# Output norm of the delta rule: square sums formed inside the scan, reciprocals on packed rows

## The reference, cut to what matters

```
def rms_norm(x, gain):
    y = xf * lax.rsqrt(jnp.mean(xf * xf, axis=-1, keepdims=True) + EPS)
    return (y * gain.astype(jnp.float32)).astype(x.dtype)

    o = gated_delta_rule(q, k, v, beta, g).transpose(0, 2, 1, 3)
    zf = z.reshape(b_, s_, GDN_HEADS, GDN_DV).astype(f32)
    o = rms_norm(o, o_gain) * jax.nn.silu(zf)
    return o.reshape(b_, s_, GDN_VDIM).astype(hn.dtype) @ w_out
```

## Time and profile before

| | us |
|---|---|
| median of 3 runs | 2438.69 (2437.46 to 2439.86) |
| profiled execution, its own time | 2455.42 |
| its span, from first to last instruction | 2453.6 |
| TensorE busy | 2096.4 (85%) |
| VectorE busy | 1113.7 (45%) |
| ScalarE busy | 697.3 (28%) |
| GpSimd busy | 319.3 (13%) |
| mean granted TensorE clock, share of full | 0.921 |

### The profile page before, as it was taken

How to read it: one execution, slowest core, us unless ns; L and a number is a source line. 1 busy time by engine, 2 the same in 40 slices (tenths; PEclk the granted TensorE clock), 3 DMA queues, 4 the chain that set the end, 5 groups by cost and what they waited for, 6 DMA issues and landing times. The chain is left out here.

```text
span 2453.6 us, 26623 instructions
## 1 busy us (share of the span) xinstructions
PE 2096.4 (85%) x10044; PEld 1566.1 (64%) x10044; DVE 1113.7 (45%) x1530; ACT 697.3 (28%) x1021; POOL 319.3 (13%) x299
## 2 busy tenths in 40 slices
PE   5988994878878996899929999997897658999999
PEld 2766762322246774788817888885675436788887
DVE  3433333111135678665483544334487343544333
ACT  2331131111124443112123322222443452422222
POOL 1331011111123430323101000000000110100000
PEclk9998696999989998899969999999998879999999
DMA  8155026999931221000002333331221002333331
GB/s 314 52 184 187 1 69 262 418 424 423 417 142 48 90 86 51 1 1 1 1 17 79 93 103 94 94 99 56 77 77 52 0 0 69 94 95 96 95 100 52
DMA packets 61937, 283.12 MB, mean 115 GB/s; under 512 B 9984, under 2 KB 11296, under 8 KB 52512
## 3 DMA queue, kind: packets, MB, share of 16 engines
q1 hardware_dynamic: 53072, 266.95, 30.9%
q0 software_dynamic: 6256, 11.03, 1.2%
q10 hardware_dynamic: 2528, 4.01, 0.5%
HBM read 280.90 MB, written 14.68 MB: 120 GB/s over the span
## 5 line engine op out<-in xcount | busy, mean ns | idle before, releaser
L307 PE MATMUL ps<-ff_hhi,ff_whi 128*128 128x512 f32 x704 | 276.9, 393 | 8.5 <-DVE ff_hlo L2486 8.3
L2404 DVE TENSOR_TENSOR ff_wlo<-ring,ff_whi 128x1024 fp32r<-128x1024 f32 x132 | 163.4, 1238 | 247.5 <-ACT ff_whi L2400 247.5
L309 PE MATMUL ps<-ff_hlo,ff_whi 128*128 128x512 f32 x704 | 275.4, 391 | 0.0
L308 PE MATMUL ps<-ff_hhi,ff_wlo 128*128 128x512 f32 x704 | 275.4, 391 | 0.0
L2400 ACT ACTIVATE ff_whi<-ring 128x1024 fp32r<-128x1024 f32 x132 | 139.2, 1055 | 321.7 <-PE ps L309 299.9
L1451 PE MATMUL ps<-w_up,hgT 128*64 128x512 f32 x576 | 145.2, 657 | 45.4 <-DMA w_up<-experts 45.4
L307 PEld LDWEIGHTS ps<-ff_hhi,ff_whi 128*128 128x128 f32 x704 | 133.2, 189 | 38.2 <-DVE ff_wlo L2404 10.2
L308 PEld LDWEIGHTS ps<-ff_hhi,ff_wlo 128*128 128x128 f32 x704 | 133.2, 189 | 28.1 <-issue 0.5
L309 PEld LDWEIGHTS ps<-ff_hlo,ff_whi 128*128 128x128 f32 x704 | 133.0, 189 | 27.9
L307 PE MATMUL ps<-ff_ahi,ff_whi 128*128 128x512 f32 x352 | 136.9, 389 | 0.0
L308 PE MATMUL ps<-ff_ahi,ff_wlo 128*128 128x512 f32 x352 | 136.9, 389 | 0.0
(11 more groups left out here) (553 smaller groups left out, 4135.1 us busy)
## 6 DMA issues: line engine op xcount, KB each, us to landing
ring<-stream SPq DMA_DIRECT2D x276, 512.0 KB, 3.6
w_up<-experts SPq DMA_DIRECT2D x36, 2048.0 KB
mix<-experts SPq DMA_DIRECT2D x18, 1024.0 KB, 19.9
hn<-experts SPq DMA_DIRECT2D x18, 1024.0 KB, 21.1
yrow<-y_dram SPq DMA_DIRECT2D x4, 1024.0 KB, 8.0
tab<-table POOLq DMA_DIRECT2D x1, 2528.5 KB, 12.3
res<-xT ACTq DMA_DIRECT2D x1, 2048.0 KB, 18.6
h_dram<-mix SPq DMA_DIRECT2D x4, 512.0 KB, 11.3
```

Of the source, the lines that this page charges most:

```text
L307: pe.matmul(out, w_hi, a_hi, start=start, stop=False)
L308: pe.matmul(out, w_lo, a_hi, start=False, stop=False)
L309: return pe.matmul(out, w_hi, a_lo, start=False, stop=stop)
L2404: ve.tensor_tensor(w_lo[:, j % 2, :], ring[:, (B0 + j) % SLOTS, :], w_hi[:, j % 2, :].bitcast(F32), ALU.subtract).then_inc(blocks_done, 1)
```

## The change

The norm's block goes away, and its work is split between the scan and a short tail behind it, in the same block.

- In the scan ScalarE reads each output chunk twice from PSUM: it writes its squares to `hctx` (`o_square`) and the output times the gain to Q.
- TensorE adds up the squares of chunk n - 1 behind the first products of chunk n (`square_sums`). It multiplies by 32 columns of ones only, and the result of chunk n goes to the partitions 32n to 32n + 31 of bank 6 + g. So the four chunks lie in four groups of 32 partitions, and a group of four heads fits one bank: 4 chunks x (4 heads x 128 tokens).
- GpSimd multiplies each finished chunk by the gate Z.
- Behind the scan VectorE has two scalings of 128x512 instead of eight, ScalarE two roots, and VectorE two reciprocals, all on `on_rows` in `sml`.
- TensorE sends the rows back: eight products, whose left operand is one column of the identity, repeated 128 times. Each picks row 32n of `on_rows` and spreads it over all partitions, into the banks of `back_bank`.
- VectorE multiplies Q by these eight results.
- ScalarE takes one root of a dummy at the start of the block.

```
+                def square_sums(n):
+                    for g in range(2):
+                        pe.wait_ge(on_sq[g], n + 1)
+                        pe.matmul(ps[32 * n:32 * n + 32, 6 + g, :], ones[:, 0:32], o_square(g, n), start=True, stop=True
+                                  ).then_inc(on_sum[g], 1)
...
+                    if n:
+                        square_sums(n - 1)
...
+                square_sums(TT - 1)
+                for i, (g, n) in enumerate(order):
+                    pe.wait_ge(on_inv, g + 1)
...
+                    if i >= 6:
+                        pe.wait_ge(on_done, i - 5)
+                    pe.matmul(ps[:, back_bank[i], :], ident[:, 32 * n:32 * n + 1].to_broadcast([P, P]), on_rows[:, g, :],
+                              start=True, stop=True).then_inc(on_back, 1)
...
+                for g in range(2):
+                    ve.wait_ge(on_sum[g], TT)
+                    ve.tensor_scalar(on_rows[:, g, :], ps[:, 6 + g, :], 1.0 / P, EPS, ALU.mult, ALU.add).then_inc(on_ms, 1)
+                for g in range(2):
+                    ve.wait_ge(on_root, g + 1)
+                    ve.reciprocal(on_rows[:, g, :], on_rows[:, g, :]).then_inc(on_inv, 1)
+                ve.wait_ge(on_gated, 2 * TT)
+                for i, (g, n) in enumerate(order):
+                    ve.wait_ge(on_back, i + 1)
+                    ve.tensor_tensor(o_part(Q, g, n), o_part(Q, g, n), by_head(ps[:, back_bank[i], :]), ALU.mult
+                                     ).then_inc(on_done, 1)
...
+            @block.gpsimd
+            def _(pool):
+                for n in range(TT):
+                    for g in range(2):
+                        pool.wait_ge(o_kept2[g], n + 1)
+                        pool.tensor_tensor(o_part(Q, g, n), o_part(Q, g, n), o_part(Z, g, n), ALU.mult
+                                           ).then_inc(on_gated, 1)
...
+                act.activation(ea[:, :], ab8[:, 0:1], ACT.Sqrt)
...
+                        act.activation(o_square(g, n), ps[:, 2 + g, :], ACT.Square).then_inc(on_sq[g], 1)
+                        act.activation(o_part(Q, g, n), by_head(ps[:, 2 + g, :]), ACT.Copy, scale=col("ogain")
                                        ).then_inc(o_kept2[g], 1)
...
-                for h in range(HEADS):
-                    act.activation(hn[:, h, :], Q[:, h, :], ACT.Square).then_inc(on_sq, 1)
...
-                    ve.reciprocal(mix[:, h, :], mix[:, h, :]).then_inc(on_step, 1)
...
-                    ve.scalar_tensor_tensor(mix[:, h, :], Q[:, h, :], col("ogain"), mix[:, h, :], ALU.mult, ALU.mult
-                                            ).then_inc(on_step, 1)
...
-                    ve.tensor_tensor(Q[:, h, :], mix[:, h, :], Z[:, h, :], ALU.mult).then_inc(on_done, 1)
```

More of the change, by code:

```diff
@@ L2220, in program, with o_square, o_part, by_head @@
             [sem(f"{n}{g}") for g in range(2)] for n in ("s_zero", "ws_done", "vn_done", "so_done", "sd_done", "o_kept2"))
-        s_next = [sem(f"s_next{g}") for g in range(2)]
+        s_next, on_sq, on_sum = ([sem(f"{n}{g}") for g in range(2)] for n in ("s_next", "on_sq", "on_sum"))
+        on_ms, on_root, on_inv, on_back, on_gated, on_done = (
+            sem(n) for n in ("on_ms", "on_root", "on_inv", "on_back", "on_gated", "on_done"))
+        on_rows = sml[:, 0:2 * T].rearrange("p (g t) -> p g t", g=2)
+        order = [(g, n) for g in range(2) for n in range(TT)]
+        back_bank = (0, 1, 4, 5, 2, 3, 0, 1)
+        def o_square(g, n):
+            b = 4 * (n % 2) + 2 * g
+            return hctx[:, b:b + 2, :].rearrange("p b t -> p (b t)")
+        def o_part(x, g, n):
+            return x[:, 4 * g:4 * g + 4, n * P:(n + 1) * P]
+        def by_head(x):
+            return x.rearrange("p (h e) -> p h e", h=4)
         with nc.Block() as block:
@@ L2246, in _ @@
                             m.then_inc(sd_done[g], 1)
+                square_sums(TT - 1)
+                for i, (g, n) in enumerate(order):
+                    pe.wait_ge(on_inv, g + 1)
+                    if i == 4:
+                        for u in range(2):
+                            pe.wait_ge(o_kept2[u], TT)
+                    if i >= 6:
+                        pe.wait_ge(on_done, i - 5)
+                    pe.matmul(ps[:, back_bank[i], :], ident[:, 32 * n:32 * n + 1].to_broadcast([P, P]), on_rows[:, g, :],
+                              start=True, stop=True).then_inc(on_back, 1)
             @block.vector
@@ L2278, in _ @@
                         act.wait_ge(so_done[g], n + 1)
-                        act.activation(Q[:, 4 * g:4 * g + 4, n * P:(n + 1) * P],
-                                       ps[:, 2 + g, :].rearrange("p (h e) -> p h e", h=4), ACT.Copy
+                        if n >= 2:
+                            act.wait_ge(on_sum[g], n - 1)
+                        act.activation(o_square(g, n), ps[:, 2 + g, :], ACT.Square).then_inc(on_sq[g], 1)
+                        act.activation(o_part(Q, g, n), by_head(ps[:, 2 + g, :]), ACT.Copy, scale=col("ogain")
@@ L2281, in _ @@
                                        ).then_inc(o_kept2[g], 1)
+                for g in range(2):
+                    act.wait_ge(on_ms, g + 1)
+                    act.activation(on_rows[:, g, :], on_rows[:, g, :], ACT.Sqrt).then_inc(on_root, 1)
         st.close()
[L2285 to L2289, removed]
-                for h in range(HEADS):
-                    act.activation(hn[:, h, :], Q[:, h, :], ACT.Square).then_inc(on_sq, 1)
[L2292 to L2308, removed]
-                    ve.reciprocal(mix[:, h, :], mix[:, h, :]).then_inc(on_step, 1)
-                    ve.wait_ge(on_step, 2 * h + 1)
-                    ve.scalar_tensor_tensor(mix[:, h, :], Q[:, h, :], col("ogain"), mix[:, h, :], ALU.mult, ALU.mult
-                                            ).then_inc(on_step, 1)
-                    ve.wait_ge(on_step, 2 * h + 2)
-                    ve.tensor_tensor(Q[:, h, :], mix[:, h, :], Z[:, h, :], ALU.mult).then_inc(on_done, 1)
```

## The result

| | us |
|---|---|
| before, median of 20 runs | 2440.02 (2437.46 to 2457.67) |
| changed, median of 20 runs | 2425.72 (2414.37 to 2434.54) |
| ratio | 0.9914, 95% interval 0.9893 to 0.9935 |
| profiled execution, before and after | 2455.42 and 2430.39 |
| span, before and after | 2453.6 and 2428.6 |

The account below looks back on a forecast made before the run. Bound: VectorE's serial chain of eight reciprocals and gain products, leaving TensorE waiting 42.3 us before the projection. Norm -31.3, scan +6.0, projection head -0.8 make -26.1: 2438.7 to 2412.6 us, range 2408 to 2419 (8 in 10).

Parts of the forecast that it names:

- the last of the sum: Whole kernel: unprofiled median stays 16.7 us below the profiled execution, so 2438.7 - 26.1 gives 2412.6 us.
- The stages behind: Stages after the projection: no change forecast; stages before and behind moving over 2 us against each other would refute it.
- head of the projection: From L307: TensorE at half clock for about 4.4 instead of 6.2 us, saving 0.8 us (ends 0 and -2.7).
- scan, three pairs: Scan: three added pairs of sum products on TensorE, 2.0 us each, paid in full, +6.0 us (5.2 to 6.8).
- norm, from t = 0 to its end: From when ScalarE can take up the scan's last output chunk: norm ends at t = 16.3 instead of 47.6, -31.3 us.
- of this, at full clock: Tail: with TensorE at full clock VectorE is last by 0.3 us and the norm ends at t = 14.4.
- of this, half clock: Tail: after 4.4 us idle TensorE runs 4.4 us at half clock, adding 1.9 us to the norm's end.
- local sum: Scan, norm and head of the projection together: -31.3, +6.0 and -0.8 make -26.1 us.
- The full clock: Rival, tail and projection head: clock stays full in both idle times, -29.9 us, 2408.8 us; chance 0.14.
- Half clock throughout: Rival, tail and projection head: clock stays half through both, -20.6 us, 2418.1 us; chance 0.18.
- The switch to 32 rows: Rival, scan: switch costs more than to 64 rows; at 4.0 us a pair 2418.6 us; chance 0.04 beyond the range.
- GpSimd's product: Rival: GpSimd's gate products become the bound, slower from 8.1 us each, 2446 us at 9 us each; chance 0.02.

## Why the prediction was wrong

**The step that failed is the last of the sum**, "The unprofiled median stands 16.7 lower, 0.7%, spread over a span that hardly changes, so I take the same difference". The 16.7 us were not spread over the span. Most of them sat in one stage at 235 to 277 us, which took the profiled execution 41.7 us at 0.50. The three runs shown have no trace; that they passed it faster is inferred, from 25.9 us in the changed kernel in its lower level and from 29.3 us in the kernel before with 3.4 us of filling. The forecast therefore took an upper-level profile against a lower-level median, which did no harm to the difference, but took for granted that the lower level would be what is measured. Eleven of the twenty runs of the changed kernel were in the upper, against four of the twenty of before, and this alone takes 9 of the 23.5 us out of the difference of the medians. In the lower level the changed kernel's median, 2416.4, is within the range and 3.8 us above the forecast. The range, built on the costs of the change alone, had no room for 16 us from elsewhere; no rival named it.

What the runs don't settle is whether the change has an influence on how often the upper level comes. Over all executions of the two unedited kernels, before was there 25 times in 77, changed 14 times in 28; on one chip 15 in 31 against 3 in 8. The stage lies ahead of the change, and chips differ as much (3 in 11, 3 in 15, 9 in 19 for the same kernel). It may be chance, and it isn't shown. Nor is it known what sends the stage to half clock in one execution and not in the next.

**The stages behind gave something back.** This term stood at nothing in the forecast, and the prediction named it as a sign of being wrong if it came to more than 2 us. The seven traces of the changed kernel whose tail is not edited need 1124.7 to 1124.8 us from the feed-forward stage to the end. The three of before (the third with the eight added products far ahead) need 1122.1, 1123.7 and 1122.0, and the one of 1123.7 had the 1.5 us less at the head of the projection (50.5 instead of 52.0). Counted from L307 to the end the scatter is gone: 1174.0 to 1174.1 in the three, 1176.2 to 1176.3 in the seven. So head and stages behind, forecast together at -0.8, are +2.2. The clearest part is one product of 512 columns of float32 after the other, before (16 records):

```profile
1697.10:1704.20 7.10, 7.10 (x16) 2.94 (x16) 0.00 (x0) 4.85 (x8) 0.00 (x0) 1.00 0.01 2
```

and after:

```profile
1669.10:1677.90 8.80, 8.79 (x16) 3.51 (x16) 0.00 (x0) 4.83 (x8) 0.00 (x0) 0.81 0.00 0
```

The idle time ahead of both is 2.4 us. In the one the clock holds to the end of the products, in the other it falls to half within them (0.65 from 1669.1 to 1674.0), and 1.7 us are lost. Another 0.7 go in the 201 products behind the next long wait (50.8 us at 0.97, 51.5 at 0.96); the rest is not placed. With the tail's filling the end takes 1121.8 and 1121.9, which is why that edit gave 7.0 us (2420.0 to 2413.1) where its own stretches account for 3.9. It is not the earlier start: two traces of the changed kernel 15.7 us apart at the scan take the same from there on. What decides it the runs don't tell.

**The terms of the sum**, each against its measurement in the profiles of the upper level:

| term | forecast | measured | from |
|---|---|---|---|
| scan, three pairs | +6.0 | +6.1 | 3 x 2.04 |
| norm, from t = 0 to its end | 47.6 to 16.3 | 47.6 to 15.4 | 1233.55, 1248.95 |
| of this, at full clock | 14.4 | 13.7 | the run with one-pass rows |
| of this, half clock | +1.9 | +1.7 | 55.3 less 53.6 with the tail filled |
| norm's end to L307 | 3.35, unchanged | 3.35 | 1248.95, 1252.30 |
| head of the projection | -0.8 | -0.5 | L307 to the feed-forward stage, 51.98 and 51.46 |
| local sum | -26.1 | -26.6 | |
| stages behind | 0 | +2.7 | 1122.1 and 1124.8 |

With the other unedited trace of before the local sum is -25.2 and the stages behind give +1.2; each pair makes 24 us less in all. The local terms were right within a microsecond. The idle time of 4.04 us (forecast 4.4) was followed by half clock only 0.8 us after the first product, and for 3.4 us instead of 4.4; then a second fall of 5.0 us in place of 4.4.

**The rivals.** The full clock did not come by itself; the run with a filled tail shows what it is worth, 1.7 us in the tail and 2.3 at the head, where the forecast had 1.9 and 1.9 (2.7 less 0.8). Half clock throughout didn't come either. The switch to 32 rows costs no more than that to 64: the last of L2250's loads starts at 1216.23 + 1.90 and the next could follow 0.11 later, at 1218.24 (the same sum gives the 1217.27 of before); the narrow one starts at 1218.44, 0.20 later, and from there to L2261 it takes 1.83, 0.11 more than two products; 0.31 in all, forecast 0.29. The Trainium skill says in "TensorEngine Tiling (Array Packing)", Key Properties, that a change of the tiling mode drains TensorE; the 0.31 us agree with that, and a drain here would be small. GpSimd's product took 1272 ns, pieces with gaps or not, and was done long before it was wanted. ScalarE's scaled copy took 682 ns instead of 600, in the shadow of TensorE.

## What to carry to other kernels

Ahead of an edit, look at the single times of the kernel, not at their median alone: if a profiled execution stands 0.7% above the runs, find out in which stage before taking its difference to them. If there are levels, compare within a level or make both kernels stay in one; here eight small products did that, and turned two medians 14.3 us apart, from 20 runs each, into two 23.7 us apart with hardly any scatter. And where rows are equal over partitions, reciprocals are to be taken on packed rows: VectorE paid 3.3 us for each 128x512, and TensorE's way back costs 0.86 for each, which can be cut to a single pass where rounded rows are precise enough.

## What the runs showed of the hardware

- TensorE that is busy for nearly all of a stage can still stay at half clock: 39.95 us busy of 41.60, and 0.50 throughout. The stage has products of 128 columns over 64 rows and of 64 columns over 64 rows beside full ones. The same stage takes 25.9 us at 0.90, in another execution.
- Eight added products of 256 columns alone left no execution in the upper level, in 21 of both kernels (11 and 10), and sixteen with 128 or with 32 columns of weights left none in 6 each. Of the 105 executions of the two unedited kernels 39 were there.
- Products added with no use can pay for themselves: seven of 0.86 us at full clock, in two idle times of 4 us, made the kernel 7.0 us shorter (2420.0 to 2413.1).
- An edit can change the time of untouched stages behind it, with the same products at another clock: from L307 to the end 1176.2 to 1176.3 us in seven traces of the changed kernel with its tail unedited, against 1174.0 to 1174.1 in three of before. Where in these stages the time goes can differ between traces of one kernel (1122.1 and 1123.7 behind the feed-forward stage's start), and their sum did not.
